# Differential attention: sums of squares over an added tile, made ready in two parts

## The chip, the cores and the metric

The kernel runs on one core of one Trainium2 chip. The metric is the device time of one execution in microseconds (us). Unless said otherwise a number is in us.

## What is computed

One sequence of 512 tokens and 2048 channels goes through a mixed block of two recurrent branches, then a latent attention layer, then a differential attention layer. Only the last is touched:

```python
def diff_layer(x, pos, layer_idx, norm_g, w_in, q_gain, k_gain, ..., subln_g, w_out):
    z = rms_norm(x, norm_g) @ w_in
    q, k, v, gate = jnp.split(z, [B_QK, 2 * B_QK, 2 * B_QK + B_WIDTH], axis=-1)
    ...
    o = diff_attend(q, k, v, pos, lam)            # 8 heads, 256 value channels each
    o = rms_norm(o, subln_g) * (1.0 - lam_init)
    return x + (o.reshape(b, s, B_WIDTH) * jax.nn.silu(gate)) @ w_out
```

The sums of squares in question are those of the second `rms_norm`: for each of 512 tokens the sum of `o * o` over the head's 256 channels.

## The kernel before

All five compute engines follow instruction streams written by hand; steps name each other by semaphores (`need(DI_ACT, "osq1")` waits for that named step of this head). SyncE loads weights in units of 1024 rows by 128 columns into four slots, GpSimd splits each into a high and a low part (L315, L319), and TensorE multiplies (L339, L340, L341: three 128x512 matmuls for each 128 rows of the contraction, which I call one group). A projected tile of 128 columns takes 16 groups; a head of the differential layer has 8 tiles (2 of q, 2 of k, 2 of v, 2 of the gate), so 128 groups.

The heads run in a loop of seven turns and one head written out behind it. A turn of TensorE's stream (`diff_pe`) interleaves the attention of head i-1 (`diff_heads_pe`) with the projection of head i: each `yield n` of `diff_heads_pe` is a place where 2n groups of the projection are put. I call these groups fill. What is left of the first 96 groups follows at once behind the attention, and `diff_scale_pe` has the last 32. In the last head the fill is the first part of the output projection (`out_ahead`, 50 groups), and what is left of it follows the attention.

Channels of a head stand on the 128 partitions, tokens along the free dimension. The attention output of a head is `diff_v`, two halves of 128 channels by 512 tokens. It comes in four blocks of 128 tokens: TensorE multiplies a block (L2440, step `V0` to `V3`), ScalarE copies it out of PSUM (L2520, `o0` to `o3`). Then ScalarE squares both halves (L2524, `osq0`, `osq1`), TensorE sums over the partitions with a column of ones (L2447, `osum`), which gives four columns of 128 tokens; VectorE makes the reciprocal root from them (L2643 and the small steps of the helper at L494 to L521), TensorE spreads it over the partitions (L1413, `oinv`), and VectorE scales, gates and stores (L2647, L2650). Only then does VectorE take the next head's tiles out of PSUM (L2576).

`diff_sq` are four scratch tiles of 128x512 floats. The first two are also the score tiles `diff_scores` (`d_sc`), used at another time of the head.

Of the kernel before, what the change touches and what calls it, by code (L numbers as in the profile page):

```python
# [7 lines left out]
ACT = mybir.ActivationFunctionType  # L8
ALU = mybir.AluOpType
# [6 lines left out]
P = 128  # L16
SEQ = 512
D_MODEL = 2048
KB = D_MODEL // P
TB = SEQ // P  # L20
# [107 lines left out]
class Steps:  # L128
# [9 lines left out]
    def done(self, name, turn=0):  # L138
        return turn * self.n + (self.order.index(name) + 2)
# [45 lines left out]
def tokens(ap, width):  # L185
    return ap.rearrange("p (c t) -> p c t", t=width)
# [18 lines left out]
def build(nc, io):  # L205
    stack = ExitStack()
    with stack:
# [4 lines left out]
        def steps(name, names):  # L212
            steps_of[name.split("_")[-1]].append(sem(name))
            return Steps(steps_of[name.split("_")[-1]][-1], names)
# [7 lines left out]
        work = [stack.enter_context(nc.psum_tensor(f"work{b}", [P, 512], F32)) for b in range(4)]  # L222
# [21 lines left out]
        ones = common[:, C_ONES:C_ONES + P]  # L244
# [282 lines left out]
        def tagged(tag):  # L527
            return " ".join(tag + s for s in RSQRT.split())
# [856 lines left out]
        def token_sums(pe, bank, block, column):  # L1385
            for b in range(TB):
                mm = pe.matmul(bank[:, bass.ds(column(b), 1)], block[:, b * P:(b + 1) * P], ones[:, 0:1],
                               start=True, stop=True)
            return mm
# [876 lines left out]
        def out2_dve(dve):  # L2266
# [13 lines left out]
            for j, before, between in ((0, range(0, 4), ()), (1, range(4, 6), ()), (2, range(6, 8), ()), (3, (), range(8, 9))):  # L2280
# [8 lines left out]
        a11 = Arena(nc, mix2_end, nc.sbuf_usable_end)  # L2289
# [8 lines left out]
        d_v = a11.take("diff_v", 2 * SEQ)  # L2298
# [2 lines left out]
        d_vt = a11.take("diff_v_tok", 2 * SEQ)  # L2301
        dist = tokens(a11.take("distances", TB * SEQ)[:, :], SEQ)
        d_sq_at = a11.at
        d_sq = [a11.take(f"diff_sq{n}", SEQ) for n in range(4)]
        d_sc = [a11.over(f"diff_scores{c}", d_sq_at + 4 * SEQ * c, SEQ) for c in range(2)]
        d_e = [a11.over(f"diff_exp{c}", d_sq_at + 4 * SEQ * (2 + c), SEQ) for c in range(2)]
        d_gt_at = a11.at
# [18 lines left out]
        dpiped = lambda *a: piped(*a, n=TB)  # L2326
# [7 lines left out]
        DP_PE = steps("dist_pe", "lam")  # L2334
        dpos_loaded = sem("dpos_loaded")
        DI_PE = steps("diff_pe", "rows sums vt0 vt1 inv0 inv1 " + dpiped("Sa{0} Sb{0}", "T{0}", "V{0}") + " osum oinv")
        DI_ACT = steps("diff_act", "sq0 sq1 sq2 sq3 rows vt0 vt1 hq0 hq1 t0 hk0 hk1 t1 " + dpiped("ea{0} eb{0}", "pT{0}", "o{0}") + " osq0 osq1")
        DI_DVE = steps("diff_dve", "ms " + RSQRT + " nsl lq0 lq1 gate0 k0 k1 lk0 lk1 gate1 " +
                       dpiped("sca{0} mxa{0} nba{0} scb{0} mxb{0} nbb{0}", "rec{0} rl{0} pb{0} p{0}", "", (1, 0)) +
                       " oms " + tagged("o_") + " og0 o0 og1 o1")  # L2340

        OUT3 = OutStage("out3", 9, U_OUT3, T_OUT3, mix2_v, xh, xl)
        AHEAD3 = ((8, 14),)
# [67 lines left out]
        def diff_heads_pe(pe, p, behind_sums=4):  # L2411
            need = lambda steps, name: pe.wait_ge(steps.sem, steps.done(name, p))
            for k in dpipe:
                if k < TB:
                    qs = slice(k * P, (k + 1) * P)
                    for c, x in enumerate("ab"):
                        if k == 0:
                            need(DI_ACT, f"vt{c}")
                            need(DI_DVE, f"lk{c}")
                        else:  # L2420
                            need(DI_DVE, f"sc{x}{k - 1}")
                        multiply(pe, work[c][:, :], dq_hi[c][:, qs], dq_lo[c][:, qs], dk_hi[c][:, :], dk_lo[c][:, :],
                                 True, True).then_inc(DI_PE.mark(f"S{x}{k}"), 1)
                    yield 3
                if 1 <= k <= TB:
                    need(DI_DVE, f"p{k - 1}")
                    if k >= 2:
                        need(DI_ACT, f"pT{k - 2}")
                    for c in range(TB):
                        cs = slice(c * P, (c + 1) * P)  # L2430
                        mm = pe.transpose(work[2][:, cs], d_p[:, cs], ident)
                    mm.then_inc(DI_PE.mark(f"T{k - 1}"), 1)
                    yield 1
                if k >= 2:
                    need(DI_ACT, f"pT{k - 2}")
                    if k >= 3:
                        need(DI_ACT, f"o{k - 3}")
                    for x in range(2):
                        for c in range(TB):
                            mm = pe.matmul(work[3][:, x * P:(x + 1) * P], d_vt[:, 256 * c + x * P:256 * c + (x + 1) * P],  # L2440
                                           d_pt[:, c * P:(c + 1) * P], start=(c == 0), stop=(c == TB - 1))
                    mm.then_inc(DI_PE.mark(f"V{k - 2}"), 1)
                    yield 1
            need(DI_ACT, "osq1")
            for b in range(TB):
                for x in range(2):
                    mm = pe.matmul(work[2][:, b:b + 1], d_sq[x][:, b * P:(b + 1) * P], ones[:, 0:1],  # L2447
                                   start=(x == 0), stop=(x == 1))
            mm.then_inc(DI_PE.mark("osum"), 1)
            yield behind_sums  # L2450
            need(DI_DVE, "o_out_")
            token_values(pe, work[3], d_small[:, 68:72]).then_inc(DI_PE.mark("oinv"), 1)
# [24 lines left out]
        def diff_heads_act(act, p, before_scores=lambda: None, split=lambda k: None):  # L2477
            need = lambda steps, name: act.wait_ge(steps.sem, steps.done(name, p))
            act.wait_ge(DI_DVE.sem, DI_DVE.after(p))
            for j, x in enumerate((d_q[0], d_q[1], d_k[0], d_k[1])):  # L2480
                act.wait_ge(tile_free, T_DIFF + 8 * p + j + 1)
                act.activation(d_sq[j][:, :], x[:, :], ACT.Square).then_inc(DI_ACT.mark(f"sq{j}"), 1)
            need(DI_PE, "rows")
            act.activation(d_vt[:, 0:SEQ], work[2][:, :], ACT.Copy).then_inc(DI_ACT.mark("rows"), 1)
            for x in range(2):
                need(DI_PE, f"vt{x}")
                act.activation(tokens(d_vt[:, :], 256)[:, :, x * P:(x + 1) * P], tokens(work[x][:, :], P), ACT.Copy)\
                   .then_inc(DI_ACT.mark(f"vt{x}"), 1)
            for c in range(2):
                act.activation(dq_hi[c][:, :], d_q[c][:, :], ACT.Copy).then_inc(DI_ACT.mark(f"hq{c}"), 1)  # L2490

            def gate_tanh_of(x):
                act.wait_ge(tile_free, T_DIFF + 8 * p + 7 + x)
                act.activation(d_gt[:, :], d_gr[:, :], ACT.Tanh, scale=0.5).then_inc(DI_ACT.mark(f"t{x}"), 1)

            gate_tanh_of(0)
            for c in range(2):
                need(DI_DVE, f"k{c}")
                act.activation(dk_hi[c][:, :], d_k[c][:, :], ACT.Copy).then_inc(DI_ACT.mark(f"hk{c}"), 1)
            before_scores()  # L2500
            gate_tanh_of(1)
            for k in dpipe:
                if k < TB:
                    for c, x in enumerate("ab"):
                        need(DI_DVE, f"nb{x}{k}")
                        if k:
                            need(DI_DVE, f"p{k - 1}")
                        act.activation(d_e[c][:, :], d_sc[c][:, :], ACT.Exp, bias=d_row[:, 2 + c:3 + c],  # L2508
                                       scale=d_small[:, 4 * c + k:4 * c + k + 1], accum_out=d_row[:, 4 + c:5 + c])\
                           .then_inc(DI_ACT.mark(f"e{x}{k}"), 1)  # L2510
                if 1 <= k < TB:
                    split(k)
                if 1 <= k <= TB:
                    need(DI_PE, f"T{k - 1}")
                    if k >= 2:
                        need(DI_PE, f"V{k - 2}")
                    act.activation(d_pt[:, :], work[2][:, :], ACT.Copy).then_inc(DI_ACT.mark(f"pT{k - 1}"), 1)
                if k >= 2:
                    need(DI_PE, f"V{k - 2}")
                    act.activation(tokens(d_v[:, :], SEQ)[:, :, (k - 2) * P:(k - 1) * P], tokens(work[3][:, 0:256], P),  # L2520
                                   ACT.Copy).then_inc(DI_ACT.mark(f"o{k - 2}"), 1)
            act.wait_ge(DI_ACT.sem, DI_ACT.so_far(p))
            for x in range(2):
                act.activation(d_sq[x][:, :], d_v[:, x * SEQ:(x + 1) * SEQ], ACT.Square).then_inc(DI_ACT.mark(f"osq{x}"), 1)  # L2524

        def diff_dve(dve):
            dve.wait_ge(h_all_summed, 1)
# [39 lines left out]
        def diff_heads_dve(dve, p, before_scores=lambda: None, behind_scores=lambda: None):  # L2567
            need = lambda steps, name: dve.wait_ge(steps.sem, steps.done(name, p))
            chain = lambda: dve.wait_ge(DI_DVE.sem, DI_DVE.so_far(p))
            done = lambda ins, name: ins.then_inc(DI_DVE.mark(name), 1)  # L2570
# [67 lines left out]
                                                      rs[:, 4 * c + k:4 * c + k + 1], ALU.mult, ALU.mult), f"nb{x}{k}")  # L2638

            behind_scores()  # L2640
            need(DI_PE, "osum")
            chain()
            done(dve.tensor_scalar(work[2][:, 16:20], work[2][:, 0:4], 1.0 / B_V, EPS, ALU.mult, ALU.add), "oms")  # L2643
# [151 lines left out]
```

## Time and profile before

| | us |
|---|---|
| median of 3 runs | 3263.66 |
| lowest and highest of them | 3259.72, 3266.76 |
| the profiled execution | 3262.1 |
| its span from the first to the last instruction | 3260.3 |
| mean granted TensorE clock | 0.990 |
| busy: TensorE, VectorE, ScalarE, GpSimd | 3195.9, 1576.2, 751.8, 2097.7 |

How to read the rows further down. PE is TensorE's matmul lane and PEld its weight loads, which overlap the matmuls; a float32 matmul that is not split by the program has two records. A row of the timeline has start, duration, engine, line, operation, written and read tiles with their shape, the count of merged instructions, and in brackets the engine's idle time before it with what ended that. Matmuls overlap, so what one costs is read from start to start. In a row of the windows, after the stretch and its length, stand busy time and count of PE, PEld, DVE, ACT and POOL, then the granted clock as a part of 2.4 GHz, then DMA share and GB/s.

### The profile page before, as it was taken

What the parts mean: (1) busy time and instruction counts of PE and PEld (TensorE: products, weight loads), DVE (VectorE), ACT (ScalarE), POOL (GpSimd) and SP (SyncE); (2) the same over time, 40 slices, a digit from 0 to 9 for tenths busy, and PEclk for the clock granted to TensorE, in tenths of its full rate; (3) what the DMA queues carried; (4) which work ended last, traced back from release to release, by engine and by line L of the source; (5) the groups of instructions that cost most, each with busy time, mean ns of one, the idle gap of its engine ahead of it and who ended that gap; (6) DMA issues with size and microseconds to landing.
All of it is one profiled execution on the core that took longest, in us unless ns stands there. A gap on an engine that the chain in (4) does not pass through costs nothing.

```text
span 3260.3 us, 58192 instructions
## 1 busy us (share of the span) xinstructions
PE 3195.9 (98%) x18914; PEld 2558.2 (78%) x18914; DVE 1576.2 (48%) x3138; ACT 751.8 (23%) x1460; POOL 2097.7 (64%) x3460
## 2 busy tenths in 40 slices
PE   8999999999999999899999999999999999999999
PEld 6777777778888777688877777887888888888777
DVE  3556666646565763731276676142344234323510
ACT  2122222223333300410144444021121112111200
POOL 6555555558787878587743344887657666666675
PEclk9999999999999999799999999999999999999999
DMA  4111111122222223233311111333222222222232
GB/s 147 54 57 55 53 53 55 57 64 83 74 81 77 71 82 92 62 93 94 88 49 35 32 48 52 97 94 89 74 71 82 79 71 71 84 77 71 65 119 88
DMA packets 459564, 239.46 MB, mean 73 GB/s; under 512 B 27901, under 2 KB 456120, under 8 KB 458936
## 3 DMA queue, kind: packets, MB, share of 16 engines
q1 hardware_dynamic: 455656, 232.19, 24.5%
q10 hardware_dynamic: 3792, 5.58, 0.5%
q8 instruction: 90, 1.47, 0.2%
q14 instruction: 26, 0.21, 0.0%
HBM read 233.52 MB, written 4.19 MB: 73 GB/s over the span
## 4 chain that ended last, share of the span: by engine, by line
PE 89%; DVE 7%; issue 2%; ACT 1%; SPq 1%; DMA 0%; DVEq 0%; POOL 0%; ACTq 0%; PEldq 0%; POOLq 0%
PE proj L339 24%; PE proj L340 23%; PE proj L341 23%; PE work L2440 2%; PE work L670 1%; PE work L678 1%; PE work L2034 1%; PE work L654 1%; PE work L339 1%; PE work L341 1%; PE work L340 1%; PE work L1171 1%; PE work L1399 1%; PE work L1413 1%; PE work L2027 1%
## 5 line engine op out<-in xcount | busy, mean ns | idle before, releaser
L315 POOL TENSOR_SCALAR w_hi<-raw_weights 128x256 fp32r<-128x256 f32 x1728 | 749.0, 461 | 1139.4 <-DMA raw_weights<-w_in 407.7
L319 POOL TENSOR_TENSOR w_lo<-raw_weights,w_hi 128x256 fp32r<-128x256 f32 x1728 | 1367.0, 825 | 0.0
L339 PE MATMUL proj<-x_hi,w_hi 128*128 128x512 f32 x2976 | 1225.9, 412 | 11.4 <-DVE x_lo L1670 6.7
L340 PE MATMUL proj<-x_lo,w_hi 128*128 128x512 f32 x2976 | 1180.9, 397 | 0.0
L341 PE MATMUL proj<-x_hi,w_lo 128*128 128x512 f32 x2976 | 1180.3, 397 | 0.0
L339 PEld LDWEIGHTS proj<-x_hi,w_hi 128*128 128x128 f32 x2976 | 562.5, 189 | 156.5 <-issue 24.8
L341 PEld LDWEIGHTS proj<-x_hi,w_lo 128*128 128x128 f32 x2976 | 561.4, 189 | 137.2
L340 PEld LDWEIGHTS proj<-x_lo,w_hi 128*128 128x128 f32 x2976 | 563.2, 189 | 117.8 <-issue 2.2
L339 PE MATMUL proj<-o_hi,w_hi 128*128 128x512 f32 x256 | 103.7, 405 | 3.6 <-DVE o_lo L1057 3.2
L340 PE MATMUL proj<-o_lo,w_hi 128*128 128x512 f32 x256 | 102.3, 400 | 0.0
L341 PE MATMUL proj<-o_hi,w_lo 128*128 128x512 f32 x256 | 102.0, 399 | 0.0
L339 PE MATMUL proj<-lat_hi,w_hi 128*128 128x512 f32 x224 | 96.1, 429 | 1.3 <-DVE lat_lo L1824 0.3
L2576 DVE TENSOR_TENSOR diff_v<-proj,diff_rinv_all 128x512 f32<-128x512 f32 x16 | 11.1, 692 | 168.1 <-PE proj L341 168.1
L340 PE MATMUL proj<-lat_lo,w_hi 128*128 128x512 f32 x224 | 88.4, 395 | 0.0
L341 PE MATMUL proj<-lat_hi,w_lo 128*128 128x512 f32 x224 | 88.3, 394 | 0.0
L2508 ACT ACTIVATE diff_exp<-diff_scores,diff_rows,diff_small 128x512 f32<-128x512 f32 x64 | 52.3, 816 | 142.4 <-DVE diff_rows L2637 142.4
L2218 DVE TENSOR_TENSOR y_group<-mix,proj 128x512 f32<-128x512 f32 x16 | 11.0, 687 | 139.6 <-PE proj L341 139.6
L2085 ACT ACTIVATE mla_exp<-mla_scores,mla_rows,mla_small 128x512 f32<-128x512 f32 x64 | 52.2, 815 | 113.3 <-DVE mla_rows L2186 113.3
L2034 PE MATMUL work<-gate_tanh,mla_v_tok 128*128 128x128 f32 x512 | 67.6, 275 | 0.0
L2440 PEld LDWEIGHTS work<-diff_probs_keys,diff_v_tok 128*128 128x128 f32 x512 | 62.0, 191 | 3.0
L2034 PEld LDWEIGHTS work<-gate_tanh,mla_v_tok 128*128 128x128 f32 x512 | 62.8, 192 | 0.7
L2440 PE MATMUL work<-diff_probs_keys,diff_v_tok 128*128 128x128 f32 x512 | 62.3, 275 | 0.0
(469 smaller groups left out, 4028.8 us busy)
## 6 DMA issues: line engine op xcount, KB each, us to landing
raw_weights<-w_in SPq DMA_DIRECT2D x260, 256.0 KB, 3.1
raw_weights<-b_w_in SPq DMA_DIRECT2D x256, 256.0 KB, 3.1
raw_weights<-a_w_in SPq DMA_DIRECT2D x100, 256.0 KB, 3.2
raw_weights<-w_out SPq DMA_DIRECT2D x64, 256.0 KB, 2.9
raw_weights<-a_w_out SPq DMA_DIRECT2D x64, 256.0 KB, 3.0
raw_weights<-b_w_out SPq DMA_DIRECT2D x64, 256.0 KB, 3.0
raw_weights<-a_w_kv_up SPq DMA_DIRECT2D x32, 256.0 KB, 2.9
mix<-x SPq DMA_DIRECT2D x4, 1024.0 KB, 8.2
```

What stands on the lines that cost most here:

```text
L315: pool.tensor_scalar(part(hi_v, s, q), part(raw_v, s, q), 1.0, 1.0, ALU.mult, ALU.mult).then_inc(hi_done, 1)
L319: pool.tensor_tensor(part(lo_v, s, q), part(raw_v, s, q), part(hi_v, s, q).bitcast(F32), ALU.subtract).then_inc(w_split, 1)
L339: pe.matmul(out, w_h, a_h, start=start, stop=False)
L340: pe.matmul(out, w_h, a_l, start=False, stop=False)
L341: return pe.matmul(out, w_l, a_h, start=False, stop=stop)
L654: mm = pe.matmul(work[banks[half]][hs, (c % 4) * P:(c % 4 + 1) * P], left[hs, c * 64:(c + 1) * 64], ar[hs, c], start=True, stop=True)
L670: mm = pe.matmul(work[0][hs, c64(c)], nb[hs, c, 0], tri[hs, c64(c)], start=True, stop=True)
L678: mm = pe.matmul(work[2][hs, c32(c)], y_m[hs, c64(c)], odd, start=True, stop=True)
L2034: mm = pe.matmul(work[2 + k % 2][:, 0:P], m_vt[h][:, cs], m_pt[k % 2][:, cs], start=(c == 0), stop=(c == TB - 1))
L2085: act.activation(m_e[k % 2][:, :], m_sc[k % 2][:, :], ACT.Exp, bias=m_row[:, 2 + k % 2:3 + k % 2], scale=m_small[:, k:k + 1], accum_out=m_ ...
L2440: mm = pe.matmul(work[3][:, x * P:(x + 1) * P], d_vt[:, 256 * c + x * P:256 * c + (x + 1) * P], d_pt[:, c * P:(c + 1) * P], start=(c == 0) ...
L2508: act.activation(d_e[c][:, :], d_sc[c][:, :], ACT.Exp, bias=d_row[:, 2 + c:3 + c], scale=d_small[:, 4 * c + k:4 * c + k + 1], accum_out=d_ ...
```

## The change

The two squared halves are added by VectorE before the sum over partitions, so that TensorE sums one tile instead of two. To have the sum early, squares and adds go by token halves: the first 256 tokens of both channel halves are squared as soon as `o1` is there, the other 256 behind `o3`. One more `yield 1` stands in front of the sum, that is two more groups of fill.

```diff
-        d_sq = [a11.take(f"diff_sq{n}", SEQ) for n in range(4)]
+        d_sqs = a11.take("diff_sq", 4 * SEQ)
+        d_sq = [d_sqs[:, n * SEQ:(n + 1) * SEQ] for n in range(4)]
...
-            need(DI_ACT, "osq1")
-            for b in range(TB):
-                for x in range(2):
-                    mm = pe.matmul(work[2][:, b:b + 1], d_sq[x][:, b * P:(b + 1) * P], ones[:, 0:1],
-                                   start=(x == 0), stop=(x == 1))
-            mm.then_inc(DI_PE.mark("osum"), 1)
+            yield 1
+            need(DI_DVE, "oadd1")
+            token_sums(pe, work[2], d_sq[0], lambda b: b).then_inc(DI_PE.mark("osum"), 1)
             yield behind_sums
...
-            act.wait_ge(DI_ACT.sem, DI_ACT.so_far(p))
-            for x in range(2):
-                act.activation(d_sq[x][:, :], d_v[:, x * SEQ:(x + 1) * SEQ], ACT.Square).then_inc(DI_ACT.mark(f"osq{x}"), 1)
+                    if k in (3, TB + 1):
+                        x = k // TB
+                        by_half = lambda v: tokens(v, SEQ)[:, :, x * 2 * P:(x + 1) * 2 * P]
+                        act.wait_ge(DI_ACT.sem, DI_ACT.so_far(p))
+                        act.activation(by_half(d_sqs[:, 0:2 * SEQ]), by_half(d_v[:, :]), ACT.Square)\
+                           .then_inc(DI_ACT.mark(f"osq{x}"), 1)
...
             behind_scores()
+            for x in range(2):
+                half = slice(x * 2 * P, (x + 1) * 2 * P)
+                need(DI_ACT, f"osq{x}")
+                done(dve.tensor_tensor(d_sq[0][:, half], d_sq[0][:, half], d_sq[1][:, half], ALU.add), f"oadd{x}")
             need(DI_PE, "osum")
```

`token_sums` (L1387) is the helper that other layers of the kernel use already: four matmuls, each with a 128x128 block of the tile as weights and one column of ones.

On TensorE, in the loop, from the last attention block (L2440, L2441 now) to the sums; before:

```order
L2440 MATMUL work3<-diff_probs_keys_222,diff_v_tok_209 128x128 x8
L339 MATMUL proj2<-x_hi0_58,w_hi_56 128x512
L340 MATMUL proj2<-x_lo0_59,w_hi_56 128x512
L341 MATMUL proj2<-x_hi0_58,w_lo_55 128x512
...
L2412 REGISTER_ALU
L2447 MATMUL work2<-common_49,diff_sq0_211 128x1
L2447 MATMUL work2<-common_49,diff_sq1_212 128x1
...
L346 ISA
```

and of the change:

```order
L2441 MATMUL work3<-diff_probs_keys_219,diff_v_tok_209 128x128 x8
L339 MATMUL proj2<-x_hi0_58,w_hi_56 128x512
L340 MATMUL proj2<-x_lo0_59,w_hi_56 128x512
L341 MATMUL proj2<-x_hi0_58,w_lo_55 128x512
...
L346 ISA
L339 MATMUL proj2<-x_hi1_60,w_hi_56 128x512
L340 MATMUL proj2<-x_lo1_61,w_hi_56 128x512
L341 MATMUL proj2<-x_hi1_60,w_lo_55 128x512
...
L2413 REGISTER_ALU
L1387 MATMUL work2<-common_49,diff_sq_211 128x1 x4
```

Two groups stood between the last block and the sums and four stand there now; the third and fourth are the first two of the next weight unit (`x_hi1`, behind the wait L346), and eight matmuls of one column have become four.

On ScalarE, the end of a head's loop turn (L2517 copies probabilities, L2520 the output); before:

```order
L2517 ACTIVATE diff_probs_keys_222<-work2 128x512
L2520 ACTIVATE diff_v_204<-work3 128x2x128
...
L2520 ACTIVATE diff_v_204<-work3 128x2x128
L2522 ISA
L2524 ACTIVATE diff_sq0_211<-diff_v_204 128x512
L2524 ACTIVATE diff_sq1_212<-diff_v_204 128x512
```

and of the change:

```order
L2518 ACTIVATE diff_v_204<-work3 128x2x128
L2523 ISA
L2524 ACTIVATE diff_sq_211<-diff_v_204 128x2x256
L2476 REGISTER_ALU x2
L2515 ACTIVATE diff_probs_keys_219<-work2 128x512
L2518 ACTIVATE diff_v_204<-work3 128x2x128
L2476 REGISTER_ALU
L2518 ACTIVATE diff_v_204<-work3 128x2x128
L2523 REGISTER_ALU
L2524 ACTIVATE diff_sq_211<-diff_v_204 128x2x256
```

One of the two squares has moved from behind the last copy to behind the second, ahead of the copy of the last block's probabilities.

## Rows read from the trace of the kernel before

**Rows 1.** The page: span, and TensorE's row of busy time.
```profile
span 3260.3 us, 58192 instructions
...
PE 3195.9 (98%) x18914; PEld 2558.2 (78%) x18914; DVE 1576.2 (48%) x3138; ACT 751.8 (23%) x1460; POOL 2097.7 (64%) x3460
```

**Rows 2.** Waits, 2290 to 3110: us in total, times, longest.
```profile
POOL w_hi L315 <- DMA raw_weights<-b_w_in: 259.2, 107, 8.0
...
PEld work L2447 <- ACT diff_sq L2524: 5.5, 8, 0.7
...
PE work L2447 <- ACT diff_sq L2524: 2.0, 8, 0.3
```

**Rows 3.** Timeline of the first head's sums, TensorE alone.
```profile
2313.21 0.40 PE L341 MATMUL proj<-x_hi,w_lo 128*128 128x512 f32 x1
2313.86 1.95 PE L2447 MATMUL work<-common,diff_sq 128*128 128x1 f32 x16 [0.25 <-ACT diff_sq L2524]
2315.67 0.48 PE L339 MATMUL proj<-x_hi,w_hi 128*128 128x512 f32 x1
...
2316.44 0.40 PE L339 MATMUL proj<-x_hi,w_hi 128*128 128x512 f32 x1
...
2320.64 0.40 PE L339 MATMUL proj<-x_hi,w_hi 128*128 128x512 f32 x1
```

**Rows 4.** Timeline of the same stretch, ScalarE and VectorE.
```profile
2301.57 1.11 DVE L2624 SCALAR_TENSOR_TENSOR diff_probs<-diff_exp,diff_rows,diff_exp 128x512 f32<-128x512 f32 x1
...
2304.53 0.38 ACT L2520 ACTIVATE diff_v<-work 128x256 f32<-128x256 f32 x1
...
2309.05 0.60 ACT L2517 ACTIVATE diff_probs_keys<-work 128x512 f32<-128x512 f32 x1 [4.14 <-PE work L2440]
...
2312.65 1.15 ACT L2524 ACTIVATE diff_sq<-diff_v 128x512 f32<-128x512 f32 x2
...
2315.93 0.17 DVE L2643 TENSOR_SCALAR work<-work 128x4 f32<-128x4 f32 x1 [13.26 <-PE work L2447]
```

**Rows 5.** Timeline of TensorE where the layer norm calls the helper once.
```profile
2187.50 0.39 PE L341 MATMUL proj<-x_hi,w_lo 128*128 128x512 f32 x1
2187.74 0.95 PE L1387 MATMUL work<-common,squares 128*128 128x1 f32 x8
2188.54 0.48 PE L339 MATMUL proj<-x_hi,w_hi 128*128 128x512 f32 x1
```

**Rows 6.** Windows: five stretches with their granted clock.
```profile
2185.00:2195.00 10.00, 10.00 (x52) 8.30 (x51) 6.29 (x20) 0.60 (x1) 10.00 (x18) 1.00 0.27 80
2315.00:2325.00 10.00, 10.00 (x50) 8.27 (x50) 4.66 (x16) 0.00 (x0) 4.30 (x8) 1.00 0.36 104
2425.00:2431.00 6.00, 6.00 (x24) 4.92 (x25) 1.84 (x11) 0.00 (x0) 3.22 (x7) 0.72 0.30 86
2647.00:2653.00 6.00, 6.00 (x23) 4.84 (x23) 1.84 (x11) 0.00 (x0) 3.42 (x7) 0.72 0.28 83
2869.00:2875.00 6.00, 6.00 (x22) 4.79 (x22) 1.84 (x11) 0.00 (x0) 3.98 (x8) 0.72 0.22 66
```

**Rows 7.** Timeline: the sums of the second and third head.
```profile
2423.93 1.95 PE L2447 MATMUL work<-common,diff_sq 128*128 128x1 f32 x16 [0.25 <-ACT diff_sq L2524]
...
2535.56 1.95 PE L2447 MATMUL work<-common,diff_sq 128*128 128x1 f32 x16 [0.25 <-ACT diff_sq L2524]
```

**Rows 8.** Groups of VectorE by form: adds and products of 128x256 floats.
```profile
L946 DVE TENSOR_TENSOR rw_tri_t<-rw_tri_t,work 128x256 f32<-128x256 f32 x40 | 16.8, 421 | 69.9 <-PE work L678 69.9
...
L1315 DVE TENSOR_TENSOR hg_tmp<-hg_tmp,hg_tmp 128x256 f32<-128x256 f32 x16 | 13.7, 892 | 0.0
```

**Rows 9.** Timeline of the last head, TensorE, from the sums on.
```profile
3090.63 0.40 PE L341 MATMUL proj<-x_hi,w_lo 128*128 128x512 f32 x1
...
3093.09 0.48 PE L339 MATMUL proj<-x_hi,w_hi 128*128 128x512 f32 x1
...
3101.14 0.47 PE L339 MATMUL proj<-x_hi,w_hi 128*128 128x512 f32 x1 [0.36 <-DVE x_lo L1057]
```

More of the change, by code:

```diff
@@ L2336, in build @@
         DI_PE = steps("diff_pe", "rows sums vt0 vt1 inv0 inv1 " + dpiped("Sa{0} Sb{0}", "T{0}", "V{0}") + " osum oinv")
-        DI_ACT = steps("diff_act", "sq0 sq1 sq2 sq3 rows vt0 vt1 hq0 hq1 t0 hk0 hk1 t1 " + dpiped("ea{0} eb{0}", "pT{0}", "o{0}") + " osq0 osq1")
+        DI_ACT = steps("diff_act", "sq0 sq1 sq2 sq3 rows vt0 vt1 hq0 hq1 t0 hk0 hk1 t1 " + dpiped("ea{0} eb{0}", "pT{0}", "o{0}").replace(" o1", " o1 osq0") + " osq1")
         DI_DVE = steps("diff_dve", "ms " + RSQRT + " nsl lq0 lq1 gate0 k0 k1 lk0 lk1 gate1 " +
                        dpiped("sca{0} mxa{0} nba{0} scb{0} mxb{0} nbb{0}", "rec{0} rl{0} pb{0} p{0}", "", (1, 0)) +
-                       " oms " + tagged("o_") + " og0 o0 og1 o1")
+                       " oadd0 oadd1 oms " + tagged("o_") + " og0 o0 og1 o1")
         OUT3 = OutStage("out3", 9, U_OUT3, T_OUT3, mix2_v, xh, xl)
```

## The prediction

> **What bounds the kernel.** I read the page first: TensorE is busy for 3195.9 of 3260.3 us [rows 1], so whatever is taken from its stream at full rate comes off the time, and work of the others counts only where TensorE waits for it. Next the waits of the stage with the eight heads. TensorE has one wait there that comes back in every head: the weight loads at L2447, the sums over partitions, wait for ScalarE's squares, eight times, up to 0.7 us [rows 2]. GpSimd, which feeds the weights, is itself waiting for DMA 107 times, 259.2 us in all [rows 2], and those DMAs wait for slots that TensorE frees: it has time to spare and follows TensorE when that gets faster. Then the timeline of that place. The reader is to see there that the last fill matmul starts at 2313.21, the first sum at 2313.86, the next fill at 2315.67 [rows 3], and that ScalarE ends its two squares at 2312.65 + 1.15 = 2313.80, 0.06 ahead of the first sum [rows 4]: the sum waits for exactly these. Last the windows, since a mean clock below one in a kernel that is 98% busy wants an explanation: behind the sums of three of the eight heads the granted clock of a stretch of 6 us is 0.72, in like stretches it is 1.00 [rows 6].
>
> **The change, part by part.**
>
> *The sums.* Fill matmuls start every (2320.64 - 2316.44) / 18 = 0.233 us [rows 3]. Around the sums it is 2315.67 - 2313.21 = 2.46 us from the last fill to the next [rows 3]: 0.65 to the first sum, of which 0.24 is the ordinary step and 0.41 the wait, and 1.81 for eight matmuls. The helper that is called now has its own row in this trace, where nothing is waited for: 2187.50 to 2187.74 to 2188.54, that is 0.24 + 0.80 = 1.04 us from fill to fill [rows 5]. So a head saves 2.46 - 1.04 = 1.42 us: 1.01 for four matmuls less, 0.41 for the wait, if that goes.
>
> *Does the wait go?* In front of the sums stand six more fill matmuls, 6 x 0.233 = 1.40 us, so TensorE comes to them at 2313.21 + 1.40 + 0.24 = 2314.85 (start of the first sum). They are no extra work: they are taken from what follows the attention, and the head has the same number of groups. The data: one square is left behind the last copy, 2312.65 + 1.15 / 2 = 2313.23, taken as 2313.27 with the full length of one instruction (the two overlap a little). Then the add of 128x256. The trace of before has no such add on `diff_sq`; the nearest rows are 0.42 us, with one operand in PSUM, and 0.89 us, with all in SBUF [rows 8]. With 0.06 for each handover, as measured from ScalarE to TensorE above, the sum may start between 2313.81 and 2314.28. Either end is before 2314.85, by 0.57 at the least, so the cost of the add does not enter; I take the upper one since its operands lie as here. Both ends give no wait.
>
> *What hides the other new work.* The earlier square goes behind the second copy, which ends at 2304.91; ScalarE's next instruction starts at 2309.05 after 4.14 us of idleness [rows 4], and the square takes about 0.6. The first add finds VectorE idle, from 2302.68 to 2315.93, 13.26 us [rows 4]; so does the second. Without that cover a head would pay up to 0.9 us twice. Total squares on ScalarE are unchanged, VectorE has 16 instructions more. Queued behind the second add on VectorE are the steps of the reciprocal root, which need the sum in any case.
>
> *What is late next.* The sum ends at 2314.85 + 0.80 = 2315.65 where it ended at 2315.67, so the root, the spread and the scaling come when they came, and TensorE comes to the spread behind the same number of fill groups. VectorE's taking of the next head's tiles does not move either. TensorE, though, is two groups further by then; tile 4 of the next head wants its PSUM bank 14 groups behind the spread instead of 16, 9.8 us in place of 11.2. In between VectorE has four operations on 128x512 tiles and the take; at 1.11 each, the longest of rows 4, that is 5.6 us. The weights are not late either, as GpSimd waits and not TensorE [rows 2]. No wait follows.
>
> *The last head* gives nothing. Its fill is short, and TensorE ends up waiting for the result of its own sums: at 3101.14 it starts after a wait for VectorE's `x_lo` [rows 9]. The sums would end at 3090.63 + 1.40 + 1.04 = 3093.07 where it is 3093.09 now [rows 9]; the chain behind them is the same, so what TensorE saves it waits. Sum of the matmul terms: 7 x 1.42 = 9.9 us.
>
> *The clock.* From the sums of the first head to those of the second it is 2423.93 - 2313.86 = 110.07 us, from there to those of the third 2535.56 - 2423.93 = 111.63 [rows 3, 7]. The 1.56 more is the fall to 1.2 GHz that the window from 2425 to 2431 shows, and there are three such, all directly behind the sums [rows 6]. What TensorE did before them: 2.46 us with a short wait and eight matmuls of a single column. Where the helper ran alone, 1.04 us of the same kind, the clock stayed at 1.00 [rows 6]. That stretch is now what every head has. I therefore expect the three falls to go, 3 x 1.56 = 4.7 us. The bounds of this term are 0 (all three stay) and 4.7.
>
> The Trainium skill, "TensorE: Matmul & The Clock Gate", section "HAM oscillation — how this bites in real kernels", speaks against this term: it puts such falls down to gaps in which the engine idles while it waits for a DMA. By that rule these three falls have another cause than the sums, nothing is gained on the clock, and the time is that of the first rival below. The trace here does not agree so far: the falls follow stretches in which TensorE had work all the time but for the short wait.
>
> *Sum.* 9.9 + 4.7 = 14.6 us. The profiled execution took 3262.1, which leaves 3247.5. The median of the runs shown is 3263.66, 1.56 above it, by chance the price of one fall; I carry that difference along: **3249.1**.
>
> **Rivals.**
>
> *The clock falls as often as before.* For it: what makes the clock fall is not known from these rows, three of eight is a matter of phase, and one example of the short stretch is thin. Against it: all three stand behind the sums and nowhere else in the stage. Only the matmul term is left: 3263.66 - 9.9 = 3253.8.
>
> *The add is as late as the squares were.* If copy, square and add with their handovers take 1 us more than I put, the 0.41 of the wait stays, and the long stretch with it: 7 x 1.01 = 7.1 us, 3256.6. Against it: 0.57 us of slack at the worst bound.
>
> *The clock falls in every head.* A head is 1.4 us shorter, so its stretches meet the clock's regulation at other moments. Eight falls in place of three cost 5 x 1.56 = 7.8 us, against 9.9: 3261.6, no change to measure.
>
> *Slower: the add is served late.* VectorE takes its queue in order, and the sum now hangs on it. A head becomes slower than before once the first sum starts behind 2314.85 + 1.42 = 2316.27, that is 2.0 us behind the worst bound. With 3 us of delay it starts at 2317.28, and seven heads lose 1.0 each: 3270.7. For it: TensorE's sum now waits behind two handovers in place of one, and in the last head the adds stand behind six further subtractions. Against it: VectorE's idle 13.26 us right there.
>
> **How the numbers follow.** Chances: forecast 0.58, clock as before 0.22, add as late as the squares 0.08, clock falls in every head 0.07, slower 0.05. Runs of before lie up to 3.9 us from their median, and the forecast may by that be as low as 3245.2; upward the range takes in the clock as before and the wait that stays, 3256.6, so 3245 to 3257. What can be told from no change here is 0.2%, 6.5 us: below 3257.1 is faster. Faster: 0.58 + 0.22 and about 0.06 of the third case, 0.86. Same: 0.07 and the rest of the third and a part of the slower case, 0.10. Slower: 0.04.
>
> **What would show it.** In the changed kernel's timeline the first sum should start 0.24 us behind the last fill, with no idle time noted, and fill should go on 0.8 us later; the wait for `diff_sq` should be gone from TensorE's list and none for VectorE's add be there. The distance of the sums from head to head should be 108.65 us in all turns, and no stretch of the stage should have a clock under 1.00. In the last head fill goes on within 0.1 us of the old time and the wait for `x_lo` grows by about 1.4. Wrong would be the forecast if the distance from head to head still alternates by 1.56 us (first rival), if TensorE waits for `oadd1`, or if GpSimd's weights come late in the dense fill behind the attention.

## The result

| | us |
|---|---|
| before, median of 5 runs | 3263.66 (3259.72 to 3266.76) |
| changed, median of 5 runs | 3246.42 (3245.55 to 3249.13) |
| ratio, with its 95% interval | 0.9949 (0.9934 to 0.9963) |
| predicted | 3249.1 (3245 to 3257) |

The changed kernel is 17.2 us faster by the medians. The profiled execution took 3247.01 us, its span 3245.2, 15.1 less than the span of [rows 1].

The page of the changed kernel, span and busy times:

```profile
span 3245.2 us, 58101 instructions
...
PE 3180.8 (98%) x18850; PEld 2547.6 (79%) x18850; DVE 1583.0 (49%) x3154; ACT 752.5 (23%) x1460; POOL 2096.4 (65%) x3460
```

TensorE has 64 matmul records less, which are the 32 matmuls taken out, and 15.1 us less of busy time. VectorE has 6.8 us more, and no wait of TensorE for its adds is in the list of waits further down. The same stretches as in [rows 3, 4], changed kernel, timeline of all engines:

```profile
2302.30 0.63 ACT L2524 ACTIVATE diff_sq<-diff_v 128x512 f32<-128x512 f32 x1
...
2306.41 0.60 ACT L2515 ACTIVATE diff_probs_keys<-work 128x512 f32<-128x512 f32 x1 [3.48 <-PE work L2441]
...
2310.01 0.63 ACT L2524 ACTIVATE diff_sq<-diff_v 128x512 f32<-128x512 f32 x1
...
2310.67 0.43 DVE L2645 TENSOR_TENSOR diff_sq<-diff_sq 128x256 f32<-128x256 f32 x1 [7.28 <-ACT diff_sq L2524]
...
2311.97 0.39 PE L341 MATMUL proj<-x_hi,w_lo 128*128 128x512 f32 x1
2312.20 0.94 PE L1387 MATMUL work<-common,diff_sq 128*128 128x1 f32 x8
2313.01 0.48 PE L339 MATMUL proj<-x_hi,w_hi 128*128 128x512 f32 x1
```

From fill to fill it is 1.04 us, where it was 2.46, and the first sum has no idle time in brackets any more. The second add ends at 2311.10, 1.1 us before TensorE's first sum. The earlier square, at 2302.30, stands in ScalarE's pause, which is still 3.48 us long behind it.

The waits of the changed kernel, 2290 to 3110:

```profile
POOL w_hi L315 <- DMA raw_weights<-b_w_in: 240.8, 106, 7.2
...
DVE diff_sq L2645 <- ACT diff_sq L2524: 74.5, 15, 7.3
...
PE proj L339 <- DVE x_lo L1057: 2.1, 2, 1.8
...
PE work L339 <- DVE diff_scores L2633: 1.7, 2, 0.9
```

TensorE's waits at the sums [rows 2] are gone; what is left stands in the last head. The windows behind the sums of the heads where the clock had fallen [rows 6], and one more stretch, in the changed kernel:

```profile
2422.00:2428.00 6.00, 6.00 (x29) 4.88 (x28) 1.79 (x11) 0.00 (x0) 4.25 (x8) 1.00 0.21 61
2639.00:2645.00 6.00, 6.00 (x29) 4.84 (x30) 1.83 (x11) 0.00 (x0) 3.94 (x8) 1.00 0.23 70
2856.00:2862.00 6.00, 6.00 (x30) 4.95 (x30) 1.84 (x11) 0.00 (x0) 3.42 (x7) 1.00 0.28 82
3037.00:3041.00 4.00, 3.41 (x9) 2.67 (x10) 2.85 (x7) 1.53 (x4) 2.75 (x4) 0.61 0.00 0
```

The three falls are gone. The sums of the first seven heads start 108.69 us apart, to 0.01, where it was 110.07 or 111.6. A new fall stands at 3037, in the last head, directly behind two waits of TensorE for `diff_scores`.

**Where the 15.1 us are.** The last fill matmul that stands ahead of the sums in the kernel before starts at 2313.21 [rows 3]; the same one of the changed kernel stands six matmuls ahead of 2311.97, at 2310.57. These 2.64 us arose ahead of any changed instruction: the helper's call of [rows 5] starts at 2185.09, 2.65 earlier, and about 1.4 of it is a clock fall at 1368 which this execution of the changed kernel happens not to have (granted clock 1.00 from 1366 to 1374, against 0.79). From this fill matmul of the first head to that of the seventh it is 665.06 before and 652.12 now, 12.94 less: 6 x 1.38 = 8.28 and three falls, 4.66. From there to the end it is 282.03 before and 282.52 now: the seventh head's stretch gives 1.42, the two waits for `diff_scores` take 0.5 more (1.66 in place of 1.14), and the rest, about 1.4, goes to the new fall. The longer waits are not the change's: in the second trace of the kernel before they are 1.61.

### The profile page after: what moved, and what is told of

It reads as the page before. It is cut to its first block, busy times and chain, and to the rows that moved or that the text cites. A ratio compares the mean times of both kernels' runs of the same rounds, so it can differ in the third digit from the quotient of the medians.

```text
span 3245.2 us, 58101 instructions
## 1 busy us (share of the span) xinstructions
PE 3180.8 (98%) x18850; PEld 2547.6 (79%) x18850; DVE 1583.0 (49%) x3154; ACT 752.5 (23%) x1460; POOL 2096.4 (65%) x3460
## 4 chain that ended last, share of the span: by engine, by line
PE 89%; DVE 7%; issue 2%; SPq 1%; ACT 1%; POOL 1%; DMA 0%; DVEq 0%; ACTq 0%; POOLq 0%; PEldq 0%
PE proj L339 24%; PE proj L340 23%; PE proj L341 23%; PE work L2441 2%; PE work L670 1%; PE work L678 1%; PE work L2034 1%; PE work L654 1%; PE work L339 1%; PE work L341 1%; PE work L340 1%; PE work L1171 1%; PE work L1399 1%; PE work L1413 1%; PE work L2027 1%
## 5 line engine op out<-in xcount | busy, mean ns | idle before, releaser
L339 PE MATMUL proj<-x_hi,w_hi 128*128 128x512 f32 x2976 | 1224.5, 411 | 12.5 <-DVE x_lo L1670 6.7
L2441 PEld LDWEIGHTS work<-diff_probs_keys,diff_v_tok 128*128 128x128 f32 x512 | 62.0, 191 | 3.0
L2441 PE MATMUL work<-diff_probs_keys,diff_v_tok 128*128 128x128 f32 x512 | 62.3, 275 | 0.0
```

Source lines behind the costliest of these rows:

```text
L339: pe.matmul(out, w_h, a_h, start=start, stop=False)
```

## The experiments

Two theories stood against each other. Mine: a head gains by the removed matmuls and the removed wait, and the clock falls because TensorE has a long stretch without full matmuls there. The rival: the falls have another cause, chance or the wait alone. All runs are ratios to the kernel before, run on the same chip.

**The kernel before again** (nothing changed).

> The kernel before with nothing but a comment added, for the spread of its clock falls. If the falls to 1.2 GHz behind the sums belong to the long stretch around them (2.46 us from fill to fill) and only their phase varies, the distance of the sums from head to head is again 110.07 us, or 111.6 where the clock fell, and at least one and at most six of eight heads show a fall directly behind the sums. If the three falls of the first trace were chance of another kind, there are none here, or they stand elsewhere in the head. Time: within 0.2% of before, either way.

Ratio 1.000 (0.9991 to 1.0009). Its windows behind the sums of the first, fourth and sixth head:

```profile
2312.00:2318.00 6.00, 6.00 (x23) 4.87 (x24) 1.84 (x11) 0.00 (x0) 2.13 (x5) 0.72 0.30 86
2644.00:2650.00 6.00, 6.00 (x22) 4.82 (x22) 1.83 (x11) 0.00 (x0) 3.58 (x8) 0.72 0.26 76
2866.00:2872.00 6.00, 6.00 (x20) 4.74 (x21) 1.83 (x11) 0.00 (x0) 4.14 (x8) 0.72 0.19 58
```

Three of eight heads again, partly others than in the first trace, all behind the sums and nowhere else in the stage. Heads take 110.07 or 111.6 us. The place is fixed, the head is not.

**More fill alone.** The edit, to the kernel before:

```diff
+            yield 1
             need(DI_ACT, "osq1")
```

> The kernel before with one more yield in front of the sums and nothing else: eight matmuls, no add. My theory: the wait goes, so a head without a clock fall takes 110.07 - 0.41 = 109.66 us; the stretch from fill to fill is 0.24 + 1.81 = 2.05 us. If the length of that stretch makes the clock fall, falls stay possible but are fewer than in before, zero to two; 7 x 0.41 = 2.9 us less plus 0 to 4.7 from the clock, so 0.1% to 0.2% faster. Rival, that the wait and not the small matmuls brings the falls: none of them here, and 7.5 us less in all. Rival, that the fill behind the sums is missed later: a head is not shorter than 110.07.

Ratio 0.9974 (0.9964 to 0.9985), 8.5 us faster. Timeline of its first head, and under it the windows behind the first and the seventh sums and in the last head:

```profile
2309.29 0.39 PE L341 MATMUL proj<-x_hi,w_lo 128*128 128x512 f32 x1
2309.52 1.84 PE L2448 MATMUL work<-common,diff_sq 128*128 128x1 f32 x16
2311.22 0.48 PE L339 MATMUL proj<-x_hi,w_hi 128*128 128x512 f32 x1
```

```profile
2311.00:2317.00 6.00, 6.00 (x29) 4.85 (x29) 1.84 (x11) 0.00 (x0) 4.31 (x8) 1.00 0.09 28
...
2969.00:2975.00 6.00, 6.00 (x29) 4.87 (x28) 1.80 (x11) 0.00 (x0) 4.31 (x8) 1.00 0.05 16
3040.00:3046.00 6.00, 5.20 (x16) 3.86 (x15) 4.58 (x10) 1.81 (x4) 3.29 (x6) 0.72 0.00 0
```

All heads take 109.58 us, 0.49 less than 110.07 (I expected 0.41), and no head has a fall behind its sums. One line thus gives half of the whole gain: 7 x 0.49 = 3.4 and three falls, 4.7, are 8.1 of the 8.5. That is more than I had expected of my theory, and no fall and about that gain is what the rival had, by which the wait brings the falls; so it stays open here whether the wait or the length had brought them. The traced execution (3251.54) is one of the faster of eight, from 3250.75 to 3256.59: that there is no fall behind the sums holds for it, and the slower ones may have had some. The last head has a fall, at the same place as the changed kernel.

**The adds without the extra fill.** The edit, to the changed kernel:

```diff
-            yield 1
             need(DI_DVE, "oadd1")
```

> The changed kernel without the extra yield: TensorE comes to the four sums 1.40 us earlier. Theory: the second square ends 0.07 before the add, the add takes 0.43 and the handover 0.06, so in the first head's terms the sum starts 0.60 behind the last fill start instead of 0.24: a wait of about 0.36 in every head, heads of 108.69 + 0.36 = 109.05 us, 7 x 0.36 = 2.5 us slower than the changed kernel in the loop. The last head is faster here, as its sums come about 1.0 us earlier and TensorE waits for their result: in all 1.5 us slower than the changed kernel. The stretch from fill to fill is 1.40 us; no clock fall. Rival, that the wait goes with the adds alone: heads of 108.69 here too.

Ratio 0.9960 (0.9946 to 0.9973). Timeline, weight loads, matmuls and the add of the first head:

```profile
2312.50 0.43 DVE L2644 TENSOR_TENSOR diff_sq<-diff_sq 128x256 f32<-128x256 f32 x1 [7.29 <-ACT diff_sq L2523]
...
2312.98 0.97 PEld L1387 LDWEIGHTS work<-common,diff_sq 128*128 128x128 f32 x8 [0.63 <-DVE diff_sq L2644]
...
2312.98 1.05 PE L1387 MATMUL work<-common,diff_sq 128*128 128x1 f32 x8 [0.19 <-DVE diff_sq L2644]
```

The sum waits for the add, heads take 109.13 us, 0.44 more than in the changed kernel (0.36 expected), without a fall. By the medians the run is 3.6 us slower than the changed kernel where I expected 1.5, by the spans of the two traces 2.0. The extra fill is what removes the wait; the adds alone don't.

**One add in place of two parts.** The edit, to the changed kernel, without the lists of step names:

```diff
-                    if k in (3, TB + 1):
...
+            act.wait_ge(DI_ACT.sem, DI_ACT.so_far(p))
+            for x in range(2):
+                act.activation(d_sq[x][:, :], d_v[:, x * SEQ:(x + 1) * SEQ], ACT.Square).then_inc(DI_ACT.mark(f"osq{x}"), 1)
...
-            for x in range(2):
-                half = slice(x * 2 * P, (x + 1) * 2 * P)
-                need(DI_ACT, f"osq{x}")
-                done(dve.tensor_tensor(d_sq[0][:, half], d_sq[0][:, half], d_sq[1][:, half], ALU.add), f"oadd{x}")
+            need(DI_ACT, "osq1")
+            done(dve.tensor_tensor(d_sq[0][:, :], d_sq[0][:, :], d_sq[1][:, :], ALU.add), "oadd1")
```

> The changed kernel, but not in two parts: both squares behind the last copy, one add of 128x512, the extra yield kept. Theory: squares end 1.23 behind their start, the add takes 0.65 to 0.75 where GpSimd is idle or not on its tile, so the sum is ready 0.02 to 0.17 us before TensorE comes to it: heads of 108.69 to 108.85 us, and no time that can be told from the changed kernel. Then the parts buy nothing while the extra fill is there. Rival, that the parts are needed: the add takes up to 1.4 us beside GpSimd's work, a wait of 0.7 us in every head, 5 us slower than the changed kernel.

Ratio 0.9950 (0.9936 to 0.9963), that of the changed kernel. Timeline of the first head:

```profile
2307.92 1.15 ACT L2522 ACTIVATE diff_sq<-diff_v 128x512 f32<-128x512 f32 x2
2309.11 0.69 DVE L2640 TENSOR_TENSOR diff_sq<-diff_sq 128x512 f32<-128x512 f32 x1 [10.62 <-ACT diff_sq L2522]
2309.88 1.09 PEld L1387 LDWEIGHTS work<-common,diff_sq 128*128 128x128 f32 x8
2310.11 0.95 PE L1387 MATMUL work<-common,diff_sq 128*128 128x1 f32 x8
```

The add ends at 2309.80, 0.08 before the first weight load, and heads take 108.69 us. With the extra fill in place the two parts buy nothing in the loop.

**One add and no extra fill.** Both edits above together: four sums, as in the changed kernel, but behind a long wait.

> Both squares behind the last copy, one add of 128x512, and no extra yield: four sums as in the changed kernel, but a long wait ahead of them. From the run with one add: it ends 1.32 us behind the start of the last fill that stands ahead of the sums here, so the first sum starts 1.4 to 1.5 behind that fill in place of 0.24, heads of 109.9 to 110.0 us without a clock fall, as long as those of before within 0.2. Stretch from fill to fill 2.3 us, of it 1.2 idle. Theory, that a long stretch with next to no columns brings the clock down, idle or not: falls behind the sums in one to four heads, as in before. Rival, that it takes eight small matmuls: none. Time: 8 to 13 us slower than the changed kernel, equal to before within 0.2% if the falls come.

Ratio 0.9993 (0.9984 to 1.0002), no difference to before, though it has 32 matmuls less. Timeline of the first head, then three windows:

```profile
2310.88 0.40 PE L341 MATMUL proj<-x_hi,w_lo 128*128 128x512 f32 x1
2312.26 1.05 PE L1387 MATMUL work<-common,diff_sq 128*128 128x1 f32 x8 [0.98 <-DVE diff_sq L2639]
2313.17 0.48 PE L339 MATMUL proj<-x_hi,w_hi 128*128 128x512 f32 x1
```

```profile
2313.00:2319.00 6.00, 6.00 (x22) 4.79 (x23) 1.84 (x11) 0.00 (x0) 3.65 (x8) 0.72 0.27 80
2644.00:2650.00 6.00, 6.00 (x23) 4.83 (x24) 1.84 (x11) 0.00 (x0) 3.38 (x7) 0.72 0.29 84
2976.00:2982.00 6.00, 6.00 (x21) 4.73 (x20) 1.74 (x11) 0.00 (x0) 4.25 (x8) 0.72 0.17 52
```

Heads of 109.90 us, and of 111.43 where the clock fell; 13.6 us above the changed kernel by the medians (8 to 13 expected). Eight small matmuls are not needed for a fall.

**Twelve and sixteen sums without a wait.** The four sums of the changed kernel made three or four times over, each overwriting the last. The edit, to the changed kernel:

```diff
+            for _ in range(2):      # 3 for sixteen
+                token_sums(pe, work[2], d_sq[0], lambda b: b)
             token_sums(pe, work[2], d_sq[0], lambda b: b).then_inc(DI_PE.mark("osum"), 1)
```

> The changed kernel with its four sums made three times over: twelve matmuls of one column and no wait. Cost 2.6 us, heads of 108.69 + 1.8 = 110.5 us without a fall, fill to fill 2.8 us, somewhat longer than the 2.46 of before. Theory, that the length of the stretch brings the falls: falls in three to five heads of eight, fewer than with sixteen. Rival, that a wait is needed: none. Time: 12.6 us slower than the changed kernel without falls, 17 to 20 with them.

> The changed kernel with its four sums made four times over (each overwrites the one before; the output is the same): sixteen matmuls of one column and no wait. Cost by the runs so far, 0.80 for four and 1.69 for eight: 3.5 us, so heads of 108.69 + 2.7 = 111.4 us without a fall. Theory, that the length of the stretch alone brings the falls: fill to fill 3.7 us, longer than in before, so falls in more heads than three of eight, each adding 1.3 to 1.6 us. Rival, that a wait is needed: no falls, all heads 111.4. Time: 19 us slower than the changed kernel without falls, 25 to 30 with them.

Ratios 1.0016 (1.0007 to 1.0025) and 1.0056 (1.0042 to 1.0070), 21.8 and 33.9 us above the changed kernel by the medians, more than the 17 to 20 and 25 to 30 I expected. I had counted seven heads, but the last one pays for its sums too: from its sums to the end it is 169.8 and 170.9 us in place of 167.9. Windows with twelve sums, then with sixteen (two of seven like ones, and the eighth head):

```profile
2426.00:2432.00 6.00, 6.00 (x21) 4.72 (x20) 1.75 (x11) 0.00 (x0) 4.14 (x8) 0.72 0.00 0
2648.00:2654.00 6.00, 6.00 (x22) 4.77 (x22) 1.83 (x11) 0.00 (x0) 4.27 (x8) 0.72 0.00 0
2760.00:2766.00 6.00, 6.00 (x22) 4.80 (x22) 1.84 (x11) 0.00 (x0) 4.26 (x8) 0.72 0.00 0
2982.00:2988.00 6.00, 6.00 (x23) 4.86 (x24) 1.83 (x11) 0.00 (x0) 4.26 (x8) 0.72 0.00 1
```

```profile
2316.00:2322.00 6.00, 6.00 (x23) 4.87 (x24) 1.83 (x11) 0.00 (x0) 4.20 (x8) 0.72 0.00 0
2429.00:2435.00 6.00, 6.00 (x23) 4.85 (x23) 1.83 (x11) 0.00 (x0) 3.90 (x8) 0.72 0.00 0
...
3110.00:3116.00 6.00, 6.00 (x34) 5.09 (x34) 3.40 (x14) 0.00 (x0) 0.00 (x0) 1.00 0.00 0
```

TensorE waits for nothing here, and the clock falls behind the sums in four and in seven of eight heads. So neither is a wait needed. In order of the stretch from fill to fill, read in each run's first head (for the kernel before from [rows 3], in both its traces the same):

| sums, wait | fill to fill | heads with a fall behind the sums |
|---|---|---|
| four, none (changed, and one add) | 1.04 | 0 and 0 |
| four, add late | 1.50 | 0 |
| eight, none | 1.93 | 0 |
| four, whole add late | 2.29 | 3 |
| eight, squares late (before, two traces) | 2.46 | 3 and 3 |
| twelve, none | 2.82 | 4 |
| sixteen, none | 3.72 | 7 |

No row has fewer falls than one with a shorter stretch, with idle and busy cases mixed. The rival of a wait and that of the eight small matmuls fall both; it is the length of the stretch between full matmuls that goes with the falls. What the clock goes by in it, these runs don't say. Nor do they separate the length from the distance of the heads, which without a fall between them grows with it (108.69, 109.13, 109.58 us in the kernels without falls behind the sums, 109.90 and more in the others), so that the moments at which the sums come shift too. And each count is that of one trace. The other executions have only their mean granted clock: it is 0.992 or 0.993 in all five of the changed kernel and in all five with the late adds, 0.991 to 0.994 in the eight with fill alone, and 0.988 to 0.992 in fifty of the kernel before. That agrees with the counts, but the ranges touch, and falls elsewhere go into the mean too.

**The last head without the extra fill.** The edit, to the changed kernel:

```diff
+            if behind_sums > 2:
                 yield 1
             need(DI_DVE, "oadd1")
```

> The changed kernel, but in the last head without the extra yield (two parts and the loop's yield kept). Theory: in the last head TensorE waits 1.8 us for x_lo at the end of the chain that starts with the sums. The sums start about 0.95 us earlier there (0.45 of wait in place of 1.40 of fill), so the wait for x_lo falls to about 0.4 with the wait for the add of 0.45 in its place: 1.0 us less in all, heads in the loop unchanged at 108.69. This is the one place where the parts can matter. Rival: the chain is not what TensorE waits for, and the end comes no earlier. Against before 0.5% faster, not to be told from the changed kernel by its time alone.

Ratio 0.9947 (0.9934 to 0.9961). Timeline of the changed kernel, then of this one, in the last head:

```profile
3077.32 0.95 PE L1387 MATMUL work<-common,diff_sq 128*128 128x1 f32 x8
...
3086.18 0.48 PE L339 MATMUL proj<-x_hi,w_hi 128*128 128x512 f32 x1 [1.78 <-DVE x_lo L1057]
```

```profile
3077.71 1.05 PE L1387 MATMUL work<-common,diff_sq 128*128 128x1 f32 x8 [0.20 <-DVE diff_sq L2646]
...
3086.66 0.47 PE L339 MATMUL proj<-x_hi,w_hi 128*128 128x512 f32 x1 [0.37 <-DVE x_lo L1057]
```

From the seventh head's sums to the end of the span it is 280.0 us in place of 280.9, both with the fall in the last head. I expected 1.0 and it is 0.9; it shows in the trace and not in the time (3246.65 against 3246.42). By its structure I hold it for the best version; no time here shows it.

## Why the prediction was right

*The bound* was right: TensorE's stream got shorter (15.1 us less of busy time) and the time followed.

*The stretch around the sums*, 1.42 us a head: measured 2.46 - 1.04 = 1.42, of which 1.38 arrives in the distance of the heads; where the 0.04 goes stays open. Its parts were mis-sized a little. I put 0.41 for the wait and 1.01 for four matmuls; with fill alone the stretch shrank by 0.53 and the four matmuls then gave 0.89. A wait costs more than its length, since the first weight load cannot run ahead: with the add late, load and matmul start both at 2312.98, with one add in time the load starts at 2309.88 and the matmul at 2310.11. The Trainium skill, "TensorE: Matmul & The Clock Gate", section "Step-by-step: what each phase is for", says that the engine pulls weight loads ahead of running matmuls; the traces agree, with 0.23 us ahead where nothing is waited for and none behind a wait.

*The add*: 0.43, near the lower bound of 0.42; I took 0.89, which changed nothing, as I had said. The slack was 1.1 us.

*What hides the rest*: right. The first square lies in ScalarE's pause, both adds in VectorE's.

*The last head gives nothing*: right in its mechanism. The wait for `x_lo` is 1.78 where it was 0.36, 1.42 more, as predicted.

*The clock term*: the three falls went, and the runs with twelve and sixteen sums show that a longer stretch brings falls without any wait. That the shorter one is what took them away is the reading that fits all the runs; the distance of the heads changed with it and was not varied by itself. The Trainium skill's rule in "TensorE: Matmul & The Clock Gate", section "HAM oscillation — how this bites in real kernels", that idle gaps bring the falls, is not the whole of it here: with sixteen sums TensorE idles nowhere near the sums, and its clock falls in seven heads.

*What I had wrong*: that no stretch of the stage would have a clock under 1.00. In the last head TensorE waits twice for `diff_scores`; before, this passed without a fall, now it has one, and so it has with fill alone and in the last version, but not with one add, with the late adds, or with twelve or sixteen sums, though all have the two waits. As far as the runs show, the change does not decide it.

*The size*: 15.1 us of span against 14.6 predicted, but in the profiled pair 2.64 of them come from ahead of the change and 0.5 are lost behind the seventh head's sums. From the first head on it is 12.5, so that the two numbers are as close as they are is partly luck. The medians differ by 17.2, with an interval from 12 to 22 us, and 14.6 lies in it. What the rest is was not separated.

## What to carry to other kernels

Look at what stands around a short matmul sequence and not only at its sum: from the last full matmul to the next one is the price, and a clock fall behind it belongs to the bill. Moving fill in front of a wait added no work here and gave half of the gain by one line, and the removed matmuls on top of it gave the other half (0.26% with the fill alone, 0.40% with the adds alone, 0.51% with both; the first two don't add up, since in the trace of each the three falls are already gone). The same matmuls removed behind a long wait gave nothing that could be measured. Where the engine later waits for the end of the same chain, as in the last head, the fill belongs behind.

## What the hardware showed

The clock of TensorE fell to 1.2 GHz (mean 0.72 over 6 us) behind stretches in which it worked all the time at matmuls of a single column, in four of eight heads at 2.82 us from full matmul to full matmul and in seven at 3.72. A fall lengthened the distance to the next head by 1.5 to 1.6 us. Which of eight like heads had one differed between two executions of the kernel before: the second, fourth and sixth, then the first, fourth and sixth. Eight one-column float32 matmuls took 1.70 us behind running matmuls and 1.81 behind a wait, four took 0.81 and 0.91.
